# Four-tile norms of a two-model transformer kernel: context part moved into the last down stage, diagonals of roots instead of scaled copies

## The reference, cut to what matters

```
first_block:   return rms_norm(h, final_norm)
modulate:      rms_norm_2(x, g) * (1 + scale) + shift
second_block:  hl = modulate(x_lat, norm_g[l, 0], mod_l[0], mod_l[1])
               hc = modulate(x_ctx, norm_g[l, 0], mod_c[0], mod_c[1])
```

## Time and profile before

| | |
|---|---|
| median of 3 runs | 1961.49 us (1960.19 to 1961.82) |
| profiled execution | 1962.88 us, span 1961.1 us |
| mean granted clock of PE | 0.948 |
| busy | PE 1822.8 us (93%), DVE 712.7, ACT 876.4, POOL 936.3 |
| DMA | 133 GB/s over the span |

### The profile page before, as it was taken

One profiled execution on the slowest core, in us unless ns is written; L12 is line 12 of the kernel. 1 busy time (PEld: TensorE's weight loads), 2 busy tenths in 40 slices (PEclk: granted clock), 3 DMA queues, 4 the chain that ended last, 5 costly groups with the idle time before them and its releaser, 6 DMA issues.

```text
span 1961.1 us, 26131 instructions
## 1 busy us (share of the span) xinstructions
PE 1822.8 (93%) x10342; PEld 1471.6 (75%) x10342; DVE 712.7 (36%) x1596; ACT 876.4 (45%) x1542; POOL 936.3 (48%) x408
## 2 busy tenths in 40 slices
PE   8999999998899998989789989999999798899998
PEld 6668887776688876878445677888878676679986
DVE  3433332145333312382465434333301343344421
ACT  4655444356554434333424524444422255556653
POOL 5646666675266666342112024444434161138876
PEclk9999999999899998999775999999999899999999
DMA  7328996543189954122000022333322431136654
GB/s 259 99 97 260 306 307 232 183 131 128 50 282 306 306 205 147 61 85 81 27 1 1 1 86 71 102 93 101 96 87 97 97 108 44 44 86 172 186 166 143
DMA packets 257419, 261.38 MB, mean 133 GB/s; under 512 B 11139, under 2 KB 201827, under 8 KB 251027
## 3 DMA queue, kind: packets, MB, share of 16 engines
q1 hardware_dynamic: 257011, 259.14, 41.9%
q10 hardware_dynamic: 288, 0.59, 0.1%
HBM read 258.66 MB, written 1.05 MB: 132 GB/s over the span
## 4 chain that ended last, share of the span: by engine, by line
PE 79%; DVE 8%; ACT 5%; DMA 4%; issue 2%; POOL 1%; SPq 1%; DVEq 0%; ACTq 0%
PE bank L347 22%; PE bank L348 21%; PE bank L349 20%; PE bank L1394 2%; PE bank L731 2%; PE bank L754 2%; PE bank L1043 2%; ACT work L1161 1%; ACT weights_high L334 1%; PE bank L1013 1%; PE bank L1745 1%; DMA work<-in_ada_w 1%; DVE work L1122 1%; PE bank L739 1%; PE bank L402 1%
## 5 line engine op out<-in xcount | busy, mean ns | idle before, releaser
L341 POOL TENSOR_TENSOR weights_low<-weights,weights_high 128x1024 fp32r<-128x1024 f32 (+1 forms) x388 | 917.7, 2382 | 913.5 <-ACT weights_high L334 913.0
L334 ACT ACTIVATE weights_high<-weights 128x1024 fp32r<-128x1024 f32 (+1 forms) x388 | 401.2, 1045 | 474.1 <-PE bank L349 141.5
L347 PE MATMUL bank<-normed_features_high,weights_high 128*128 128x256 f32 (+1 forms) x1408 | 441.7, 314 | 3.9 <-DVE normed_features_low L509 2.6
L349 PE MATMUL bank<-normed_features_low,weights_high 128*128 128x256 f32 (+1 forms) x1408 | 436.2, 310 | 0.0
L348 PE MATMUL bank<-normed_features_high,weights_low 128*128 128x256 f32 (+1 forms) x1408 | 436.2, 310 | 0.0
L347 PE MATMUL bank<-weights_high,normed_features_high 128*128 128x512 f32 (+4 forms) x752 | 291.7, 388 | 21.4 <-DVE normed_features_low L509 8.4
L347 PEld LDWEIGHTS bank<-normed_features_high,weights_high 128*128 128x128 f32 x1408 | 268.7, 191 | 56.3 <-issue 36.2
L349 PEld LDWEIGHTS bank<-normed_features_low,weights_high 128*128 128x128 f32 x1408 | 268.7, 191 | 14.0
L348 PEld LDWEIGHTS bank<-normed_features_high,weights_low 128*128 128x128 f32 x1408 | 268.9, 191 | 13.6
L349 PE MATMUL bank<-weights_low,normed_features_high 128*128 128x512 f32 (+4 forms) x752 | 276.7, 368 | 0.0
L348 PE MATMUL bank<-weights_high,normed_features_low 128*128 128x512 f32 (+4 forms) x752 | 276.1, 367 | 0.0
(11 more groups left out here) (299 smaller groups left out, 2073.6 us busy)
## 6 DMA issues: line engine op xcount, KB each, us to landing
work<-in_ada_w SPq DMA_DIRECT2D x48, 1024.0 KB, 8.1
weights<-in_ffn_w_up SPq DMA_DIRECT2D x44, 1024.0 KB, 6.3
weights<-in_ffn_up SPq DMA_DIRECT2D x44, 1024.0 KB, 6.0
weights<-in_ffn_w_down SPq DMA_DIRECT2D x20, 1024.0 KB, 5.1
weights<-in_ffn_down SPq DMA_DIRECT2D x20, 1024.0 KB, 5.0
weights<-in_diff_w_qkv SPq DMA_DIRECT2D x12, 1024.0 KB, 5.0
weights<-in_hyb_w_in SPq DMA_DIRECT2D x11, 1024.0 KB, 5.2
weights<-in_odd_w_in SPq DMA_DIRECT2D x9, 1024.0 KB, 5.3
```

Source lines behind the costliest of these rows:

```text
L334: A.eng.activation(high(whigh[:, m % HIGHS, :]), raw(wslot[:, u % SLOTS, :]), ACT.Copy).then_inc(scalar_done, A.one(("A", "high", m)))
L341: G.eng.tensor_tensor(raw(wlow[:, u % SLOTS, :]), raw(wslot[:, u % SLOTS, :]), high(whigh[:, m % HIGHS, :]).bitcast(F32), ALU.subtract).th ...
L347: T.eng.matmul(out_, lh, rh, start=first, stop=False)
L349: return T.eng.matmul(out_, lh, rl, start=False, stop=last)
```

## The change

Three things, and what they need.

1. The context half of 2.0 norm is made in the phase "1.1 ffn down". DVE makes the context's rstd at its start (`context_stats_V`, ACT `context_root_A`), then two 128 x 128 diagonals of the roots (`context_diag_V`); PE turns and scales the two context tiles at once by 16 float32 products of a token tile with a diagonal (`context_turn_T`, before the half f0 = 6); DVE and ACT make features, high and low parts (`context_V`, `context_A`).
2. "1 final" is gone. DVE writes the tokens times `final_norm` to `work` (`gained_tokens_V`), ACT sums the squares both of the raw and of these tokens (`last_down_A`), and one root serves both norms; the gain is multiplied into the columns of 2.0 norm (`veccol[:, 80:88]`, one more small load). The final tokens themselves are scaled later (`final_tokens_V`). The latent half takes the two-tile form (`front_V`, `front_A`), and in `first_cut_T` PE runs the first cut over the context tiles first, with the second half of the transposes and the spread between its halves, and then over the latent tiles.
3. 2.0 norm2 and 2.1 norm take a form for four tiles (`wide_T`, `wide_V`, `wide_A`): diagonals of the roots, 4 products of a token tile with a diagonal per feature tile k, the first four k ahead, the others between the products of the first cut; ACT applies gain and shift to the context half and DVE to the latent half in place in PSUM. These two phases have no fence, and the third half of weights is rounded after k = 3.

```diff
+        def context_turn_T(T):
+            T.eng.wait_ge(vector_done, done("V", "context", "diag"))
+            for k in range(KT):
+                for j in range(2):
+                    i = T.eng.matmul(context_k(k)[:, j * P:(j + 1) * P], xt[:, j, k * P:(k + 1) * P], context_diag(j), start=True, stop=True)
+            i.then_inc(tensor_done, T.one(("T", "context", "turned")))
...
+        def wide_turn_T(T, ph, k):
+
+            if k >= 4:
+                T.eng.wait_ge(vector_done, done("V", ph, "low", k - 4))
+            for j in ALL:
+                i = T.eng.matmul(wide_k(k)[:, j * P:(j + 1) * P], xt[:, j, k * P:(k + 1) * P], diag(j), start=True, stop=True)
+            i.then_inc(tensor_done, T.one(("T", ph, "turned", k)))
+
+        def wide_T(T, ph, x_ph):
+
+            T.eng.wait_ge(scalar_done, done("A", x_ph, "squares", 3))
+            warm_T(T, 0 if x_ph.endswith("out") else 4, 10)
+            T.eng.wait_ge(vector_done, done("V", ph, "diag"))
+            T.eng.wait_ge(scalar_done, done("A", ph, "diag"))
+            for k in range(4):
+                wide_turn_T(T, ph, k)
+
+        def wide_V(V, ph, x_ph, which):
+
+            V.eng.wait_ge(scalar_done, done("A", x_ph, "squares", 7))
+            rstd_V(V, ph, ALL)
+            for j in (0, 2):
+                V.eng.tensor_scalar(diag(j), ident, stat[:, 24 + j:25 + j], None, ALU.mult).then_inc(vector_done, V.one(("V", ph, "diag")))
+            for k in range(KT + 1):
+                if k < KT:
+                    a, b = which(k, 1)
+                    V.eng.wait_ge(scalar_done, done("A", ph, "context", k))
+                    V.eng.tensor_scalar(wide_k(k)[:, SEQ:2 * SEQ], wide_k(k)[:, SEQ:2 * SEQ], a, b, ALU.mult, ALU.add).then_inc(vector_done, V.one(("V", ph, "features", k)))
+                if k >= 1:
+                    q = k - 1
+                    V.eng.wait_ge(scalar_done, done("A", ph, "high", q))
+                    V.eng.tensor_tensor(nTl[:, q, :], wide_k(q), nTh[:, q, :].bitcast(F32), ALU.subtract).then_inc(vector_done, V.one(("V", ph, "low", q)))
...
+        def first_cut_T(T, ph, normed, x_ph, cuts, pieces):
...
+            T.eng.wait_ge(vector_done, done("V", "context", "low", KT - 1))
+            for tiles in (CTX, LAT):
+                for h4 in range(4):
+                    if tiles is CTX:
+                        taken.append(take_half(T))
...
+                    if tiles is CTX and h4 == 0:
+                        turn_x_T(T, normed, x_ph, 1)
+                    if tiles is CTX and h4 == 1:
+                        spread_T(T, normed)
...
+                    if ph == "1.1 ffn down" and half == 0 and f0 == 6:
+                        context_turn_T(T)
+                    if ph == "1.1 ffn down" and half == 1 and f0 == 0:
+                        T.eng.wait_ge(vector_done, done("V", "context", "low", KT - 1))
...
+        def gained_tokens_V(V, ph, c):
+            V.eng.wait_ge(vector_done, V.n)
+            for j, t in enumerate(LAT):
+                V.eng.tensor_tensor(gained(j, c), xt[:, t, 512 * c:512 * c + 512], final_g[:, 512 * c:512 * c + 512], ALU.mult).then_inc(vector_done, V.one(("V", ph, "gained", 2 * c + j)))
...
-        phase("1 final", None, final_V, final_A)
...
+            (vrows[80:88, :], rows(io["final_norm"])),
```

More of the change, by code:

```diff
@@ new lines, in context_V @@
+        def context_V(V, which):
+            V.eng.wait_ge(tensor_done, done("T", "context", "turned"))
+            for k in range(KT + 1):
+                if k < KT:
+                    a, b = which(k, 0)
+                    V.eng.tensor_scalar(context_k(k), context_k(k), a, b, ALU.mult, ALU.add).then_inc(vector_done, V.one(("V", "context", "features", k)))
+                if k >= 1:
+                    q = k - 1
+                    V.eng.wait_ge(scalar_done, done("A", "context", "high", q))
+                    V.eng.tensor_tensor(nTl[:, q, span(CTX)], context_k(q), nTh[:, q, span(CTX)].bitcast(F32), ALU.subtract).then_inc(vector_done, V.one(("V", "context", "low", q)))
@@ new lines, in context_A @@
+        def context_A(A, k):
+            A.eng.wait_ge(vector_done, done("V", "context", "features", k))
+            A.eng.activation(nTh[:, k, span(CTX)], context_k(k), ACT.Copy).then_inc(scalar_done, A.one(("A", "context", "high", k)))
+        WIDE_FRONTS = ("2.0 norm2", "2.1 norm")
+        wide_k = lambda k: psum[4 + k % 4][:, :]
+        diag = lambda j: spread[:, j * P:(j + 1) * P]
+        def wide_turn_T(T, ph, k):
[4 more added lines that the diff above has]
+            i.then_inc(tensor_done, T.one(("T", ph, "turned", k)))
@@ new lines, in wide_A @@
+        def wide_A(A, ph, x_ph, which, next_ph):
+            rstd_A(A, ph, ALL)
+            A.eng.wait_ge(scalar_done, A.n)
+            for j in (1, 3):
+                A.eng.activation(diag(j), ident, ACT.Copy, scale=stat[:, 24 + j:25 + j]).then_inc(scalar_done, A.one(("A", ph, "diag")))
+            for k in range(KT + 1):
+                if k < KT:
+                    a, b = which(k, 0)
+                    A.eng.wait_ge(tensor_done, done("T", ph, "turned", k))
+                    A.eng.activation(wide_k(k)[:, 0:SEQ], wide_k(k)[:, 0:SEQ], ACT.Identity, bias=b, scale=a).then_inc(scalar_done, A.one(("A", ph, "context", k)))
+                if k >= 1:
+                    q = k - 1
+                    A.eng.wait_ge(vector_done, done("V", ph, "features", q))
+                    A.eng.activation(nTh[:, q, :], wide_k(q), ACT.Copy).then_inc(scalar_done, A.one(("A", ph, "high", q)))
+                    if q % 4 == 3:
+                        ahead(A, first_half[next_ph] + HIGHS - 1 + q // 4)
@@ L865, in in_T @@
                     wh, wl, m = take_half(T)
+                    if c == 0 and normed in WIDE_FRONTS:
+                        for kk in range(4):
+                            k = 4 * h4 + kk
+                            T.eng.wait_ge(vector_done, done("V", normed, "low", k))
+                            for p in mine:
+                                tok = slice(p["t"] * P, (p["t"] + 1) * P)
+                                i = product(T, psum[p["bank"]][:, 0:b - a], (nTh[:, k, tok], nTl[:, k, tok]), (wh[:, kk, :], wl[:, kk, :]), k == 0, k == KT - 1)
+                                if k == KT - 1 and p is not mine[-1]:
+                                    i.then_inc(tensor_done, T.one(("T", ph, "piece", p["n"])))
+                            if kk == 3:
+                                half_read(T, i, m)
+                                if k == KT - 1:
+                                    T.note(("T", ph, "piece", mine[-1]["n"]))
+                            if k < 4:
+                                wide_turn_T(T, normed, k + 4)
+                            yield
+                        continue
                     for p in mine:
@@ L2133, in mix_V @@
             def mix_V(V):
[L2134 to L2136 removed]
+                if nm in WIDE_FRONTS:
+                    wide_V(V, nm, mixed, which)
                 else:
```

173 lines of the change are left out of this document (127 added, 46 removed).

## The result

The changed kernel took 1944.93 us (median of six executions, 1931.71 to 1947.00) beside 1960.84 us for the kernel before (six, 1957.99 to 1964.76): a ratio of 0.990, 95% interval 0.9883 to 0.9921. It is faster by about 16 us. I had given 1938.0 with a range of 1934 to 1946, so the sign and the range hold, but a third of the forecast gain is missing: the forecast of 1934.5 to 1940.5, to which I gave 0.63, did not come true. The profiled execution took 1944.56 us (span 1942.7, mean clock 0.954), 18.3 us under the profiled 1962.88 of before, where my sum said 23.4.

The account below looks back on a forecast made before the run. TensorE, 79% of the chain, was taken as the bound, with time to gain where it waits or runs at lower clock. 14.0 + 4.5 + 4.9 = 23.4 us off the profiled 1962.88, adjusted to the median, gave 1938; range 1934 to 1946.

Parts of the forecast that it names:

- Passage 1: Norm between 1.1 down and 2.0 in: 21.8 us for 40.26, less work added in the down stage, net -14.0 us.
- the prediction is wrong if the down stage grows by more than 5 us: Failure sign for the 1.1 down stage, where added diagonal products (3.6 us) and early transposes (0.9 us) were reckoned.
- The waits for POOL: In passage 1, PE idles 1.7 and 1.1 us for the third and fourth weight low parts.
- The rule by which they would have been 0.4: Transposing 4 times faster for FP32: diagonal products at 0.4 us, gain some 8 us; rival at 0.41, 1953 us, chance 0.04.
- Passage 2: Norm into 2.0 ffn up: diagonals and ten idle products start the second hidden tile at 1185.4, not 1189.88; net -4.5 us.
- Passage 3: Norm into 2.1 in: same pieces, lower clock for the first 2 to 4 us; net -4.9 us.
- Sum: Whole kernel: the three passages' gains, 14.0 + 4.5 + 4.9 = 23.4 us, taken off the time before.
- given back in 2.0 in: Rival: gained time lost in 2.0 in, where DVE's gate scans hold PE; 3 us, 1941 us, chance 0.15.
- a fallen clock in passages 1 and 2: Rival: new short gaps lower the clock, costing 3.4 us once in each passage; 1945 us, chance 0.12.
- a context norm that PE waits for: Rival: context norm not hidden, PE waits in the down stage, up to 8 us; 1946 us, chance 0.04.

Follow-up runs that it names:

- tokens_first: The changed kernel with token products before context products in the first cut of passage 1; 1936.98 us median, profiled execution 1951.56 us.
- wide_nowarm: The changed kernel without the ten idle products ahead of the diagonal products of passages 2 and 3; 1944.27 us.
- wide_morewarm: The changed kernel with 14 idle products in passage 2 and 32 in passage 3 in place of ten each; 1939.28 us, ratio 0.9887.
- warm_att: The changed kernel with two idle 128-column products at the end of each step of TensorE's attention loop; 1971.81 us, ratio 1.006.
- warm_heads: wide_morewarm with idle products added in mLSTM, 20 at its head and 12 in each later head; 1934.62 us, ratio 0.9861.
- wideonly: The kernel before with only passages 2 and 3 changed to the diagonals of roots, passage 1 as before; 1949.37 us, ratio 0.9939.
- before_heads: The kernel before with idle products in mLSTM, 20 at its head and 12 in each later head; 1953.87 us, ratio 0.9968.

## Why the prediction was right, and where it was not

**Passage 1: right in its net, with both terms about 1 us larger than reckoned.** Over all profiles, nine with the new order and four with the old, the passage takes 21.6 to 21.7 us against 39.9 to 42.8 (mean 41.2), and the stretch of 1.1 down 69.4 to 69.8 against 63.7 to 65.1 (mean 64.2). That is -19.5 and +5.4, net -14.1; I had -18.5, +4.5 and -14.0. I had also written that the prediction is wrong if the down stage grows by more than 5 us. It grew by 4.3 in the profiled pair and by 5.4 in the means, so by the means that sign stands. The added work isn't what exceeds it: the diagonal products take 3.49 us there and the transposes 0.79, 4.3 together. The rest goes with the clock: 4.1 to 5.1 us of half clock in the new down stages and 1.9 to 2.8 in three of the four old ones (4.9 in the profile that I had read). The waits for POOL were 1.76 and 0.50 us, for 1.7 and 1.1. The diagonal products cost what L414's did: the 16 in the down stage leave 32 records of 0.275 us, from 715.4 to 718.9, 0.226 us a product. The rule by which they would have been 0.4 (the Trainium skill, TensorE: Matmul & The Clock Gate, Terms) doesn't hold here: eight transposes took 1.04 us with their tail (L426 above), eight products with theirs would take some 1.95, a factor of 1.9 to 2.3. tokens_first shows what the context products cover: 5.9 us, some 2 of them half clock.

**Passage 2: right.** 27.5 became 22.9 (-4.6 for -4.5); PE stood 1.62 us for 1.4; the clock held, and without the idle products it would not have (wide_nowarm).

**Passage 3: right in size, by errors that cancel.** 34.2 became 29.4 (-4.8 for -4.9), PE stood 5.62 us for 5.5. The half clock lasted about 6.8 us by narrow stretches, 5.0 of them with PE at work, and not 2 to 4, and the 16 diagonal products lost 2.4 us and not 1.6; the products behind them were a little cheaper than my 16 us (15.16). wide_morewarm gives the price of the fall: 2.0 us.

**The step that failed is "Sum".** It adds 14.0, 4.5 and 4.9, which is 23.5 as measured over the profiles, and holds everything between them at its old time. In the profiled pair the terms make 24.1 us; the part from the spread of -M to the end of 2.0 out grew from 212.3 to 219.7 us, which takes 7.4 off, and 1.1 down happened to start 1.6 earlier: 18.3. The rival "given back in 2.0 in" was looking in the wrong stage: 2.0 in kept its 127.5 us, its 5.4 us wait included. I read the clock only in the passages and didn't see that some 130 us of mLSTM and attention, with none of the changed code, ran at a mean near 0.64 in the kernel before (0.76 from 950 to 1016, 0.51 from 1016 to 1078). A range that leans on such a stretch has to carry its 7 us.

**The range held by luck.** Its upper part, from 1940.5 to 1946, was there for rivals that didn't happen: a fallen clock in passages 1 and 2 (1945) and a context norm that PE waits for (1946). The clock was 1.00 through both passages, and PE didn't wait in the down stage. 1944.93 came from stages that no rival named. I also took 4 us for what a measurement tells from no change; single executions of the changed kernel differ by 18.

**What was shown and what stays open.** Shown: mLSTM alone takes 58.0 or 67.6 us with the same instructions, with the clock as the difference (warm_att's trace); held at full clock it takes 54.7 (warm_heads); the longer length appears without the changed passage 1 (wideonly), and in attention without any of the change (before_heads), so it isn't a price of the moved work; in the traces each passage term holds alone as together. Not shown: what picks the length. In favour of chance: the changed kernel has both kinds in 18 executions, and the kernel before has, once in 61, 1946.64 us with a clock of 0.959. In favour of something in the program: the kernel before was traced twice at 212.3 us and lies from 1956.5 to 1965 in 55 of its 61 times, where the changed kernel has two kinds, and tokens_first came out short five times in five without a profile. The Trainium skill (TensorE: Matmul & The Clock Gate, Part 1) says that the chip's look at TensorE's activity runs free and isn't reset when a kernel starts; executions and programs would then differ by where their stages fall in it. No run here tests that.

The gain in medians is 15.6 us (1959.89 over 61 times, 1944.28 over 18), 18.5 in means (1959.90 and 1941.42), 17.3 with the clock held in mLSTM, and 23.5 in the passages' own rows. The 5 to 8 us between the last and the others are the clock's in the one traced pair; in the medians that isn't shown. Holding the clock in mLSTM on both sides should have brought the medians to 23.5 if that stage were all, and brought them to 17.3: some 6 us of the shortfall stay open.

## What to carry to other kernels

Reckon a change from the rows of its own stretch, but then ask of every long stretch behind it whether it ran at full clock; one that doesn't has more than one length, and several us either way belong in the range. Where the times of a kernel fall into groups, a trace of one group can't be weighed against the median of another: cut the spans at the same instructions and compare stretch by stretch. And before shaving waits of one or two us, look for the stage in which TensorE waits briefly at half clock again and again: twelve idle products a head gave about 10 us in the traced executions here, as much as passages 2 and 3 together, and 5 to 6 in the medians (wide_morewarm to warm_heads, and the kernel before to before_heads).

## What the runs showed of the hardware

- Idle products held the clock in one stage and not in another. In mLSTM 12 a head, in a wait of 2.0 us, kept it at 1.00 with PE busy 49.33 of 55 us (warm_heads). In attention PE was busy 88.00 of 88 us and was granted 0.50 all the same (warm_att), while 20 us of the same loop's later part, with 20.00 busy, had 1.00 (the changed kernel). The Trainium skill (TensorE: Matmul & The Clock Gate, Part 1) has it that "activity releases the throttle"; the attention rows don't bear that out, and no run here tells what sets the two parts apart.
- Executions of one program differ by 17 to 18 us, and the mean granted clock with them: the changed kernel from 1929 (0.964) to 1947 (0.953), tokens_first from 1935 (0.964) to 1952 (0.951).
- Stages ahead of the changed ones scatter too. Over the fourteen profiles the first down product of layer 0 of model 1 starts anywhere from 319.2 to 323.3, and the first 1.1 down product from 703.95 to 710.03.
